# Two blocks on one core: the attention pairs of layer 0 in mixed order, one context query tile's pair and then two latent ones

## The reference, cut to what matters

```
# _token_mixer, rope is None -> the context sequence; else the latent one
o_d = _diff_attention(dq, dk, dv, lam)     # 4 heads, each two score maps
o_g = _gqa_attention(gq, gk, gv)           # 8 query heads on 2 key heads

def _diff_attention(dq, dk, dv, lam):
    s = einsum('bqhjd,bkhjd->bhjqk', dq, dk) * ATTN_SCALE
    p = softmax(s, axis=-1)
    return einsum('bhqk,bkhe->bqhe', p[:, :, 0] - lam * p[:, :, 1], dv)

def _gqa_attention(gq, gk, gv):
    p = softmax(einsum('bqhgd,bkhd->bhgqk', gq, gk) * ATTN_SCALE, axis=-1)
    return einsum('bhgqk,bkhd->bqhgd', p, gv)
```

## Time and profile before

| | |
|---|---|
| median of 3 runs | 4073.88 us (4068.94 to 4074.25) |
| profiled execution, its own time | 4068.01 us |
| its span, first to last instruction | 4066.1 us |
| PE busy / PEld / DVE / ACT / POOL | 93% / 64% / 46% / 20% / 25% |
| mean granted clock of TensorE | 0.975 |
| attention0, first score to last scaled result | 1436.0 to 1634.2 us of the span, 4.9% |

### The profile page before, as it was taken

One profiled execution on the slowest core, in us unless ns is written; L12 is line 12 of the kernel. 1 busy time (PEld: TensorE's weight loads), 2 busy tenths in 40 slices (PEclk: granted clock), 3 DMA queues, 4 the chain that ended last, 5 costly groups with the idle time before them and its releaser, 6 DMA issues. The chain is left out here.

```text
span 4066.1 us, 47766 instructions
## 1 busy us (share of the span) xinstructions
PE 3796.0 (93%) x18222; PEld 2586.0 (64%) x18222; DVE 1878.8 (46%) x3491; ACT 832.8 (20%) x1685; POOL 1013.1 (25%) x876
## 2 busy tenths in 40 slices
PE   6978969999989989999999999999999999989998
PEld 4866745555465557555555555555787767768887
DVE  3345332222322256688554566654225655243445
ACT  2123321111111156210213000001213521220001
POOL 1301200000004300222333222322152034443443
PEclk9988979999999999999999999999999999989999
DMA  5420169999811100122221223221110022212221
GB/s 206 169 80 17 63 264 396 388 395 394 343 61 55 47 12 1 60 80 101 74 105 42 93 105 120 108 93 62 47 63 32 1 72 74 92 62 83 83 90 56
DMA packets 72013, 476.62 MB, mean 117 GB/s; under 512 B 8240, under 2 KB 9648, under 8 KB 18288
## 3 DMA queue, kind: packets, MB, share of 16 engines
q1 hardware_dynamic: 68576, 462.86, 30.3%
q0 software_dynamic: 2640, 8.65, 0.7%
q10 hardware_dynamic: 576, 2.10, 0.1%
HBM read 469.38 MB, written 4.19 MB: 116 GB/s over the span
## 5 line engine op out<-in xcount | busy, mean ns | idle before, releaser
L921 PE MATMUL ps<-projected,weight_ring 128*128 128x384 f32 (+1 forms) x672 | 245.8, 521 | 0.0
L3425 PE MATMUL ps<-projected,weight_ring 128*128 128x384 f32 (+1 forms) x768 | 223.0, 434 | 1.2 <-DVE mlp_u L3624 0.6
L2325 DVE SCALAR_TENSOR_TENSOR sb_x_all<-ps,sb_modulation_ada,sb_x_all 128x512 f32<-128x512 f32 x144 | 106.4, 749 | 245.7 <-PE ps L2161 215.9
L921 PEld LDWEIGHTS ps<-projected,weight_ring 128*128 128x128 f32 x672 | 127.7, 190 | 106.1 <-issue 45.9
L3425 PEld LDWEIGHTS ps<-projected,weight_ring 128*128 128x128 f32 x768 | 144.8, 190 | 62.5 <-issue 3.0
L1307 DVE TENSOR_REDUCE attention_shift<-ps 128x1 f32<-128x768 f32 (+1 forms) x160 | 131.0, 845 | 75.7 <-PE ps L1195 75.4
L3425 PE MATMUL ps<-projected,mlp_weight_sums 128*128 128x384 f32 x480 | 165.8, 489 | 0.0
L2848 DVE SCALAR_TENSOR_TENSOR projected<-projected,sb_vectors 128x497 f32<-128x497 f32 (+26 forms) x270 | 157.9, 649 | 1.6
L3425 PE MATMUL ps<-h2b,weight_ring 128*128 128x384 f32 (+1 forms) x512 | 152.5, 442 | 6.2 <-ACT h2b L834 6.2
L1195 PE MATMUL ps<-projected 64*128 64x256 f32 (+1 forms) x576 | 136.0, 527 | 23.5 <-DVE projected L1336 15.0
L2708 PE MATMUL ps<-projected,gate_sums 128*128 128x384 f32 (+1 forms) x512 | 150.2, 437 | 5.1 <-POOL gate_sums L2988 5.1
(11 more groups left out here) (666 smaller groups left out, 7739.1 us busy)
## 6 DMA issues: line engine op xcount, KB each, us to landing
weight_ring<-w_stream SPq DMA_DIRECT2D x218, 1024.0 KB, 4.9
expert_weights<-w_moe SPq DMA_DIRECT2D x125, 1024.0 KB, 23.5
weight_ring<-w_moe SPq DMA_DIRECT2D x40, 1024.0 KB, 24.6
h2b<-w_moe SPq DMA_DIRECT2D x33, 1024.0 KB, 23.8
weight_ring<-w_stream SPq DMA_DIRECT2D x16, 512.0 KB, 3.7
weight_ring<-w_stream SPq DMA_DIRECT2D x16, 384.0 KB, 3.3
sb_x_all<-xT SPq DMA_DIRECT2D x1, 3072.0 KB, 13.3
tokens<-h_tokens ACTq DMA_DIRECT2D x4, 512.0 KB, 9.8
```

Source lines behind the costliest of these rows:

```text
L921: ins = nc.tensor.matmul(core.ps[:, 2 * slot + half, 0:n], w_of(k), h_of(k)[:, a:a + n], start=(first and k == 0), stop=(last and k == chu ...
L2325: v.scalar_tensor_tensor(core.x[:, k, NCTX:T], ps[:, bank, :], core.mods["ada"][:, 40 + k, 1:2], core.x[:, k, NCTX:T], ALU.mult, ALU.add). ...
L3425: ins = nc.tensor.matmul(acc, wq[:, k, :], bq[:, k, :], start=(first and k == 0), stop=(last and k == 3), skip_group_check=True)
```

## The change

`second_block` reorders the list for layer 0: short pair 0, long pairs 0 and 1, short pair 1, long pairs 2 and 3, and so on, 16 triples. Nothing is added to or taken from the computation, and the pairs themselves stay the same. `copy_turned` on ACT gets one more wait: where pair p-2 has fewer keys than pair p (the second long pair of each triple), the copy would overwrite `factor(p-2)`, so it waits until the result of pair p-2 was scaled.

```
@@ attention_phase, copy_turned on ACT
                 if p >= 2:
                     act.wait_ge(o_done, turns[p - 2])
+                    if pairs[p - 2]["keys"] < pairs[p]["keys"]:
+                        act.wait_ge(o_out, p - 1)
                 nc.scalar.activation(prob_t[:, 2 * (p % 2) + i, 0:n], flat_t[:, 0:n], ACT.Copy) \
                     .then_inc(pt_act, 1)
@@ second_block
+                if not last:
+                    short, long = pairs[0:CT * KD], pairs[CT * KD:]
+                    pairs = [pr for i in range(len(short)) for pr in (short[i], long[2 * i], long[2 * i + 1])]
                 attention_phase(core, f"attention{layer}", pairs, neg_lambda=neg_lam[:, :])
```

## The result

The change makes the program slower, by about the least that can be told: 4076.81 us median (4072.31 to 4085.77, 18 runs) against 4070.22 (4065.32 to 4074.91, 18 runs). The medians are 6.6 us apart. The ratio is 1.0018 with a 95% interval of 1.0011 to 1.0026, which is +7.3 us (4.5 to 10.6), where 5.4 was forecast, and inside the 0.2% that the forecast called no change.

What follows compares the result with a forecast made beforehand. PE's waits within rounds were taken as the bound: 12.4 + 23.0 + 24.0 + 70.0 + 61.3 = 190.7, with a 12.8 us drain 203.5 against 198.1 us, so 4073.88 + 5.4 = 4079.3 us, range 4069 to 4087.

Steps and rivals of the forecast that it cites:

- The bound: Layer 0's attention: PE's waits within rounds set the time; short pairs leave only 0.13 to 0.16 us beyond long ones.
- Short round behind diff pairs: Short score with a long diff pair's transposes: the mixing is not hidden, 3.26 us, or 3.31 with gqa values.
- Short round behind gqa pairs: Short score with a long gqa pair's transposes, which wait for ACT's copies: 3.44 us, or 3.42 with gqa values.
- Rounds A and B: Rounds of a triple's first and second long score: 15 A at 4.59 or 4.75 us, 14 B at 4.20 to 4.61.
- Added wait: ACT's copy for each triple's second long pair waits for the short pair's scaling, 16 times; claimed to cost nothing.
- The fill: Start of layer 0's attention: 12.4 us for the first four scores, with the low clock lasting 3.4 us.
- the sign: Start of the phase: clock back at 1.00 by 1440; the forecast is wrong if PEclk is low beyond 1443.
- The rival of the lasting low clock: Fill: clock stays at 0.50 for 16 us or more, making the change cost 11.4 us, 4085.3 us; chance 0.13.
- The other signs: Transposes 1.3 to 1.4 us after short scores behind diff pairs; ACT's copy delays gqa ones; three rounds 12.0 to 12.8 us.
- The last sign of being wrong: On ACT: the forecast is wrong if copies wait for the scaling, L1336.
- Drain: End of the phase, last score to last result: 12.8 us instead of 13.9, saving 0.44 of transposes and 0.64 of values.

Runs made afterwards that it cites:

- the longer copy: Changed kernel with ACT's copy of the first 512 columns of each long gqa map in four instructions instead of one; phase 208.2 us.
- the second profile: The changed kernel profiled once more, unaltered, to see whether its fill's low clock recurs; phase 203.65 us, 6.6 us at the low clock.

## Why the prediction held, and where it was off

**The bound.** That PE's waits in a round decide, and not its busy share, was right. 33.5 of 39 us against 148 of 159 looked like room; the room was low clock, and 0.13 to 0.16 us in a round.

**Short round behind diff pairs.** Forecast 3.26 and 3.31, measured 3.25 and 3.42, seven rounds 23.4 us for 23.0. The cause is shown by leaving the mixing out: 0.71 us each.

**Short round behind gqa pairs.** Forecast 3.44 and 3.42, by the values that the round holds; measured 3.54 and 3.28, seven rounds 24.0 for 24.0. The forecast let an exponential hold the first copy by the same amount each time. In four rounds, which follow rounds of 4.27, it held it longer; in three, which follow rounds of 4.54, it ends as the first transposes do, and PE waits only once, 0.29 us, for the second copy. The two cancel, so that the sum is exact is luck. That both copies are on the path is shown by the longer copy.

**Rounds A and B.** A without its first round 65.6 for 65.4. B 60.3 for 61.3: with diff long pairs behind and gqa ones ahead they were 4.27, not 4.49 and 4.61. I had let the next transposes wait for the 1.50 us that the row gives for the values, but the end of a matmul's row overlaps the next one's start: the transposes began 1.34 after (1477.39 to 1478.73), and the score followed 0.75 after them, not 0.81.

**Added wait.** Nothing forecast, nothing measured in the steady rounds.

**The fill.** The step that was mis-sized. To the fifth score I had 12.4 us and measured 12.1, but by two misses that cancel: the fourth score came 6.8 us after the first, not 8.0, and the round after it took 5.25, not 4.4. And I let the clock stay up from 3.4 us on. It fell a second time, and the round of the fifth score took 7.44 us in place of 4.59. Of the 2.0 us by which the phase missed the forecast (205.5 for 203.5) this is 2.85, and the smaller terms give the rest back. In the second profile that round took 5.03, and the phase 203.65. The forecast had named the sign: PEclk low beyond 1443, 7 us after the first score. It was low from 8 to 18 us after it. The rival of the lasting low clock was half right: not 16 us from the start, but a second stretch. It came in all four profiles that have this order with the mixing and the values in their place, and not in the one without the mixing. That points to the bare mixing in the fill as its cause, but it rests on one profile, and is not shown. The remark that a transpose does not count as busy in the way of a matmul (the Trainium skill, "TensorE: Matmul & The Clock Gate", Part 4: PE-mode transpose) is neither shown nor refuted by it, since without the mixing the clock stayed up through 9 us with transposes of the same shapes in them.

**The other signs.** Three came: the transposes 1.34 us behind the short score, released by the mixing; ACT's copy as the one that releases those of long gqa pairs; three rounds together 12.1 to 12.9 us. The last sign of being wrong, copies that wait for the scaling, did not.

**Drain.** From the last score to the last result: 12.8 forecast, 12.7 measured.

## What to carry to other kernels

Mixing short and long items in a pipeline written out by hand covers a short item's waits only if the long item's side work fits behind a short item's lead; here a 1.02 us mixing stood behind a 0.63 us score, 7 times, and the one set of transpose banks did the same for the others. Before reordering items, write down for each round which neighbour's step it holds and what that step waits for: round times summed in this way came to 173.7 us for 42 rounds at full clock, measured 173.3, with single rounds off by up to 0.34 us in ways that partly cancelled. And look at the order of steps within a round first: moving the values ahead of the transposes, in both layers, paid 12 us, where reordering the items of one layer lost 7.

## What the hardware showed that I had not expected

TensorE's clock fell again soon after its first return. In the changed kernel's fill it was 0.50 from 1452 to 1461, with PE busy for 7.84 of these 9 us, after PE had been busy for 2.44 of the 4 us ahead, most of them at 1.00. The wait of 1.46 us before the first long transposes ran from 1451.22 to 1452.68, so more than half of it came after the fall. In the second profile of the same kernel the clock held longer: it was 1.00 from 1443.5 to 1449.5, though PE was busy for only 2.89 of these 6 us, and fell right after. In the kernel without the mixing PE was busy for 2.89 of the 4 us that lie as far behind its first score (1446.87 to 1450.87), for 2.67 of those from 1448 to 1452 and for 7.80 of the 9 us after, and the clock stayed at 1.00 to the end of the phase. What tips it is not settled by these runs.
